# Layer 1's mixer in a decoder trunk: rows turned once, queries interleaved with compression, compressed heads summed in the turned result

## The reference

```python
s = modulate(rmsnorm(h, norm_kv), shift, scale)
kv = (s @ w_kv).reshape(B, S, 6, N_KV_GROUPS_B, HEAD_DIM)
k_cmp = rmsnorm(compress(kv[:, :, 0], pe_k, w_ck1, w_ck2), k_gains[0])
v_cmp = compress(kv[:, :, 1], pe_v, w_cv1, w_cv2)
k_sel = apply_rope(rmsnorm(kv[:, :, 2], k_gains[1]), cos, sin)   # v_sel, k_win, v_win likewise
proj = u @ w_in            # u: the same rows, other modulation
q = rmsnorm(proj[..., :hd].reshape(B, S, N_HEADS_B, HEAD_DIM), q_gain)
gates = jax.nn.sigmoid(proj[..., hd:] + b_gate).reshape(B, S, N_HEADS_B, 3)
q_rot = apply_rope(q, cos, sin)
p_cmp = jnp.where(vis, jax.nn.softmax(jnp.where(vis, logits, -1e30), axis=-1), 0.0)
o = gates[..., 0:1] * o_cmp + gates[..., 1:2] * o_sel + gates[..., 2:3] * o_win
return o.reshape(B, S, hd) @ w_o
```

## Time and profile before

| | |
|---|---|
| median of 3 runs | 1534.42 us (1533.08 to 1534.97) |
| profiled execution | 1527.08 us, its span 1525.4 us |
| PE busy | 1413.6 us (93%) |
| DVE, ACT busy | 328.9 us (22%), 266.6 us (17%) |
| DMA | 512.30 MB, mean 336 GB/s |
| mean granted clock of PE | 0.964 of full speed |

### The profile page before, as it was taken

How to read it: one execution, slowest core, us unless ns; L and a number is a source line. 1 busy time by engine, 2 the same in 40 slices (tenths; PEclk the granted TensorE clock), 3 DMA queues, 4 the chain that set the end, 5 groups by cost and what they waited for, 6 DMA issues and landing times.

```text
span 1525.4 us, 20445 instructions
## 1 busy us (share of the span) xinstructions
PE 1413.6 (93%) x8345; PEld 807.5 (53%) x8345; DVE 328.9 (22%) x774; ACT 266.6 (17%) x512; POOL 30.5 (2%) x77
## 2 busy tenths in 40 slices
PE   4999899999999999999797878889999999999997
PEld 1677766545444554444285757765454444544442
DVE  0330523211111111111132359232111111111111
ACT  2211513111111111111114236221111111111110
POOL 4000001000000000000000000010000000000000
PEclk7999999999999999999898959789999999999999
DMA  9999189599999999999976300124999999999996
GB/s 354 421 420 396 53 358 408 206 380 421 421 420 421 420 421 421 421 421 420 420 287 265 121 0 1 38 88 161 380 421 421 420 421 421 420 421 421 421 421 258
DMA packets 71311, 512.30 MB, mean 336 GB/s; under 512 B 8208, under 2 KB 8400, under 8 KB 9264
## 3 DMA queue, kind: packets, MB, share of 16 engines
q1 hardware_dynamic: 70272, 509.64, 81.3%
q0 software_dynamic: 800, 1.25, 0.4%
q10 hardware_dynamic: 144, 0.08, 0.0%
HBM read 509.89 MB, written 1.05 MB: 335 GB/s over the span
## 4 chain that ended last, share of the span: by engine, by line
PE 78%; DMA 13%; DVE 5%; ACT 2%; issue 1%; SPq 1%; DVEq 0%; ACTq 0%
PE PS L813 19%; PE PS L477 13%; DMA ring<-in_w_exp 11%; PE PS L803 10%; PE PS L821 10%; PE PS L836 9%; PE PS L498 3%; PE PS L865 2%; DMA ring<-in_w_ada_units 2%; PE PS L419 1%; PE PS L605 1%; PE PS L460 1%; DVE scratch L651 1%; DVE stats L654 1%; PE PS L904 1%
## 5 line engine op out<-in xcount | busy, mean ns | idle before, releaser
L813 PE MATMUL PS<-ring,scratch 128*32 128x512 f32 (+2 forms) x2176 | 359.3, 600 | 22.0 <-DMA ring<-in_w_exp 20.4
L813 PEld LDWEIGHTS PS<-ring,scratch 128*32 128x32 f32 (+2 forms) x2176 | 113.6, 123 | 261.3 <-issue 259.5
L477 PE MATMUL PS<-ring,uT 128*128 128x256 f32 x960 | 214.6, 383 | 1.9 <-ACT uT L443 1.1
L803 PEld LDWEIGHTS PS<-scratch,u 128*128 128x128 f32 x1600 | 183.2, 192 | 39.3 <-issue 37.4
L477 PEld LDWEIGHTS PS<-ring,uT 128*128 128x128 f32 x960 | 182.2, 192 | 34.0 <-issue 6.3
L803 PE MATMUL PS<-scratch,u 128*128 128x128 f32 x1600 | 192.4, 278 | 1.4 <-ACT scratch L1023 1.4
L821 PE MATMUL PS<-ring,scratch 128*32 128x512 f32 (+2 forms) x1088 | 182.2, 596 | 1.2 <-DVE item_first_i L1141 1.2
L836 PE MATMUL PS<-scratch 128*128 128x512 f32 x400 | 180.1, 593 | 0.0
L1156 DVE TENSOR_TENSOR scratch<-PS,gate_row 128x512 f32<-128x512 f32 x100 | 69.1, 691 | 446.7 <-PE PS L821 446.7
L1031 ACT ACTIVATE scratch<-PS 128x256 f32<-128x256 f32 x50 | 19.2, 383 | 676.0 <-PE PS L813 676.0
L821 PEld LDWEIGHTS PS<-ring,scratch 128*32 128x32 f32 (+2 forms) x1088 | 52.4, 122 | 123.1 <-issue 121.5
(11 more groups left out here) (301 smaller groups left out, 769.0 us busy)
## 6 DMA issues: line engine op xcount, KB each, us to landing
ring<-in_w_exp SPq DMA_DIRECT2D x384, 1024.0 KB, 21.1
ring<-in_w_ada_units SPq DMA_DIRECT2D x56, 1024.0 KB, 14.8
ring<-in_w_in_a_units SPq DMA_DIRECT2D x12, 1024.0 KB, 23.9
ring<-in_w_cmp_units SPq DMA_DIRECT2D x8, 1024.0 KB, 26.4
ring<-in_w_sh_units SPq DMA_DIRECT2D x6, 1024.0 KB, 9.9
ring<-in_w_kv_b_units SPq DMA_DIRECT2D x6, 1024.0 KB, 21.9
ring<-in_w_o_a_units SPq DMA_DIRECT2D x4, 1024.0 KB, 8.5
ring<-in_w_in_b_units SPq DMA_DIRECT2D x4, 1024.0 KB, 6.2
```

Source lines behind the costliest of these rows:

```text
L477: mm = pe_.matmul(PS[:, bank, t * UC:(t + 1) * UC], lhs[:, k, t * P:(t + 1) * P], w[:, k, :], start=(k == 0), stop=(k == KC - 1))
L803: mm = pe_.matmul(PS[:, bank, i * w:(i + 1) * w], u[:, t, k * P:(k + 1) * P], hot[:, t, :], start=(t == 0), stop=(t == NT - 1))
L813: mm = pe_.matmul(PS[places, GU, :], x[:, kk, places], gate_and_up, start=(kk == 0), stop=(kk == KC - 1))
```

## The change

- The normed rows are turned once. The keys' modulation writes `uT`; the queries' reads the same four banks and writes over `u` (`u_queries`), after all four banks are turned.
- Units are loaded and used in the order kv 0 to 3, compression 0 to 3, kv 4 and 5, compression 4 to 7, q 0 to 3. Plain and rotated queries are turned unit by unit (`turn_plain`, `turn_rotated`, four transpositions each), plain ones into `uT`, rotated ones into `qT`; DVE norms and rotates unit by unit. `dve_rope` handles both row tiles in one set of six operations.
- The gates' product comes after the last q unit.
- Scores and weights of the compressed branch are computed by DVE beside attention's batches 0 and 3, both row tiles at once, their exponentials by ACT after batch 1; each weight takes its gate with it. PE turns the probabilities with batches 6 and 7.
- The first branch's heads are written to `u` instead of being added. After attention `pe_turn_and_add` turns `u` by products with the identity, and adds the compressed heads in the same banks: eight products of 32 rows, 128x256 each.
- The masks `visible` and `hidden_mask` are made before the first kv unit's result is read.

```diff
-    order += [("kv", j) for j in range(6)] + [("cmp", j) for j in range(8)]
-    order += [("q", j) for j in range(4)] + [("out_b", j) for j in range(4)] + [("shared1", j) for j in range(3)]
+    order += [("kv", j) for j in range(4)] + [("cmp", j) for j in range(4)] + [("kv", 4), ("kv", 5)]
+    order += [("cmp", j) for j in range(4, 8)] + [("q", j) for j in range(4)] + [("out_b", j) for j in range(4)] + [("shared1", j) for j in range(3)]
...
+        def pe_turn_and_add(pe_, src, ready, what, added):
+            pe_.wait_ge(*ready)
+            for b in range(KC // 2):
+                for k in (2 * b, 2 * b + 1):
+                    place = PS[:, b, (k % 2) * SEQ:(k % 2 + 1) * SEQ]
+                    for t in range(NT):
+                        pe_.matmul(place[:, t * P:(t + 1) * P], src[:, t, k * P:(k + 1) * P], ident[:, :],
+                                   start=(k % 2 == 0 and t == 0), stop=False, skip_group_check=True)
+                    mm = added(k, place)
+                mm.then_inc(rows_turned, 1)
+            pe_.wait_ge(rows_copied, 4 * COPIED.index(what) + 4)
+
...
-        def act_modulate(done, what, v):
+
+        def act_modulate(done, what, v, dst=uT, in_place=False):
             done.eng.wait_ge(vectors_ready, 1 + [0, 1, 1, 2, 2][MODULATED.index(what)])
             for b in (0, 2):
-                done.eng.wait_ge(rows_turned, 4 * TURNED.index(what) + b + 1)
+                done.eng.wait_ge(rows_turned, 4 * TURNED.index(TURNED_FOR[what]) + (4 if in_place else b + 1))
...
+            kv(0)
+            pe_modulated(pe_, "mix1")
+            kv(1)
+            kv(2)
+            turn_doubled(0)
+            kv(3)
+            turn_doubled(1)
+            compress(0)
+            pe_.wait_ge(sem("kv_doubled"), 2)
+            kv(4)
             sum_tiles(0)
-            compress(1, 0)
-            compress(1, 1)
+            turn_doubled(2)
+            pe_.wait_ge(sem("kv_doubled"), 1)
+            kv(5)
+            compress(1)
+            turn_doubled(3)
+            pe_.wait_ge(sem("kv_doubled"), 3)
+            queries(0)
+            sum_tiles(1)
+            pe_.wait_ge(nsa_params, 16 * 2)
             pe_.wait_ge(sem("cmp_hidden"), 2)
             pe_.wait_ge(sem("kv_values"), 2)
...
-            compress(1, 2)
+            pe_.wait_ge(sem("kv_values"), 1)
+            queries(1)
             pe_.wait_ge(sem("cmp_k_normed"), 1)
...
                           ident[0:G * NB, 0:G * NB]).then_inc(sem("cmp_k_turned"), 1)
-            compress(1, 3)
-            sum_tiles(1)
+            pe_.wait_ge(sem("kv_copied"), 18)
+            turn_plain(0)
+            pe_.wait_ge(sem("kv_doubled"), 4)
+            queries(2)
+            turn_rotated(0)
+            turn_plain(1)
             pe_.wait_ge(sem("cmp_rep"), 2)
-            pe_.wait_ge(sem("kcz_ready"), 2)
...
-
-            pe_.wait_ge(sem("kv_doubled"), 4)
-            pe_.wait_ge(sem("kv_values"), 2)
+            pe_.wait_ge(sem("q_normed"), 1)
+            queries(3)
+            turn_rotated(1)
+            turn_plain(2)
             pe_.wait_ge(sem("kcz_ready"), 2)
-            pe_turn_rows(pe_, u, normed_rows("mix1"), "mix1")
-            pe_modulated(pe_, "mix1")
+            pe_narrow(pe_, w_gates, 6, u_queries, 3 * H, sem("gates_out"))
+            turn_plain(3)
+            turn_rotated(2)
+            turn_rotated(3)
+            pe_.wait_ge(sem("gates_active"), 1)
             pe_.wait_ge(sem("cmp_v_read"), 1)
-            pe_narrow(pe_, w_gates, 6, uT, 3 * H, sem("gates_out"))
-            for j in range(4):
-                pe_rows_unit(pe_, AT["q", j], j, uT)
-                if j == 0:
-                    pe_.wait_ge(sem("gates_active"), 1)
-                    pe_narrow_rows(pe_, narrow_T[0:3 * H, :], narrow_rows(6, SEQ, 3 * H)).then_inc(sem("gates_turned"), 1)
-            pe_turn_rows(pe_, q_rows, (sem("q_normed"), 4), "q")
...
+            def turn_cmp_probs(b):
+                t = b - CMP_TURNED_AT
+                if t in range(NT):
+                    pe_.wait_ge(sem("cmp_probs"), 1)
+                    return pe_.transpose(cmp_probs_turned(b), cmp_buf[:, t].rearrange("p h n -> p (h n)"), ident[:, :])
+
+            pe_.wait_ge(sem("rotated_copied"), 4)
             pe_attention(pe_, "nsa", nsa_batches, lambda br, pair: kT_b[:, br, pair // 2, :],
-                         lambda br, kt, hd: v_b[:, br, kt, hd // HPG, :])
-            pe_turn_rows(pe_, u, (sem("nsa_o"), 16), "nsa_o")
+                         lambda br, kt, hd: v_b[:, br, kt, hd // HPG, :],
+                         [(sem("cmp_shifted"), 1), (sem("gates_ready"), 1)], turn_cmp_probs)
+
+
+            def compressed_heads(k, bank):
+                rows = slice(32 * (k // 4), 32 * (k // 4) + 32)
+                return pe_.matmul(bank, v_diag[rows, 2 * (k % 4):2 * (k % 4) + 2, :].rearrange("p h d -> p (h d)"),
+                                  cmp_T[rows, :], start=False, stop=(k % 2 == 1), skip_group_check=True)
+
+            pe_turn_and_add(pe_, u, (sem("nsa_o"), 8), "nsa_o", compressed_heads)
...
+            act_head_squares(done, "kvn", 0, AT["kv", 2], KV_BANK[2], squares_kv)
+            to_compress(0)
+            values_of_branch(0)
+            to_compress(1)
             compressed(0)
+            act_head_squares(done, "kvn", 1, AT["kv", 4], KV_BANK[4], squares_kv)
             hidden_of(0)
+            keys_of_branch(0)
+            values_of_branch(1)
+            compressed(1)
+            keys_of_branch(1)
+            query_norm(0)
             act.wait_ge(sem("cmp_k"), 1)
             done(act.activation(kc_rows[0:G * NB, 0, :], PS[0:G * NB, 6, 0:DH], ACT.Square,
                                 accum_out=small[0:G * NB, 72:73]), sem("cmp_k_sq"))
             act.wait_ge(sem("cmp_k_mean"), 1)
             done(act.activation(small[0:G * NB, 74:75], small[0:G * NB, 73:74], ACT.Sqrt), sem("cmp_k_root"))
-            act_table(act, ACT.Silu)
-            compressed(1)
             hidden_of(1)
-            act_modulate(done, "mix1", OF_LAYER[1] + SH_M)
+            query_norm(1)
+            copy_plain(0)
+            query_norm(2)
+            copy_rotated(0)
+            copy_plain(1)
+            query_norm(3)
+            copy_rotated(1)
+            copy_plain(2)
             act.wait_ge(sem("gates_out"), 1)
             done(act.activation(narrow_T[0:3 * H, :], PS[0:3 * H, 6, 0:SEQ], ACT.Sigmoid, bias=bias_gate[:, :]),
                  sem("gates_active"))
-            for j in range(4):
-                act_head_squares(done, "qn", j, AT["q", j], j)
-            act_copy_turned(done, qT, "q")
+            copy_plain(3)
+            copy_rotated(2)
+            copy_rotated(3)
             act_table(act, ACT.Exp)
-            act.wait_ge(sem("cmp_shifted"), NT)
-            done(act.activation(cmp_buf, cmp_buf, ACT.Exp), sem("cmp_exp"))
-            act.wait_ge(sem("cmp_probs_turned"), 1)
-            done(act.activation(cmp_T[0:H * NB, :], PS[0:H * NB, 7, 0:SEQ], ACT.Copy), sem("cmp_probsT"))
-            act_copy_turned(done, qT, "q_rotated")
-            act_attention(done, "nsa", nsa_batches)
+
+            def cmp_exp(b):
+                if b == 1:
+                    act.wait_ge(sem("cmp_shifted"), 1)
+                    done(act.activation(cmp_buf, cmp_buf, ACT.Exp), sem("cmp_exp"))
+
+            act_attention(done, "nsa", nsa_batches, cmp_exp)
...
+            rotate(0)
+            query_norm(2)
+            rotate(1)
...
+            query_norm(3)
+            rotate(2)
+            rotate(3)
...
+            def cmp_scores():
+                dve.wait_ge(sem("cmp_logits"), 1)
+                done(dve.tensor_tensor(cmp_buf, cmp_logits, seen, ALU.mult))
+                done(dve.tensor_tensor(cmp_buf, cmp_buf, hidden_mask[:, :, :].unsqueeze(2).to_broadcast(of_heads), ALU.add))
+                done(dve.tensor_reduce(cmp_stat, cmp_buf, AX.X, ALU.max))
+                done(dve.tensor_tensor(cmp_buf, cmp_buf, cmp_stat.unsqueeze(3).to_broadcast(of_heads), ALU.subtract),
+                     sem("cmp_shifted"))
+
+
+            def cmp_weights():
+                dve.wait_ge(sem("cmp_exp"), 1)
+                done(dve.tensor_reduce(cmp_stat, cmp_buf, AX.X, ALU.add))
+                done(dve.reciprocal(cmp_stat, cmp_stat))
+                done(dve.tensor_tensor(cmp_stat, cmp_stat, gates[:, :, :].rearrange("p t (h b) -> p t b h", b=3)[:, :, 0, :],
+                                       ALU.mult))
+                done(dve.tensor_tensor(cmp_buf, cmp_buf, seen, ALU.mult))
+                done(dve.tensor_tensor(cmp_buf, cmp_buf, cmp_stat.unsqueeze(3).to_broadcast(of_heads), ALU.mult),
+                     sem("cmp_probs"))
+
+            def beside_attention(b):
+                if b == 0:
+                    cmp_scores()
+                elif b == 3:
+                    cmp_weights()
...
             def nsa_finish(b, heads, rinv):
                 br, t, g = nsa_batches[b]
```

(10 more changed lines are left out.)

336 lines of the change are left out of this document (173 added, 163 removed).

## The result

| | before | changed |
|---|---|---|
| median | 1534.7 us (1533.08 to 1535.22) | 1508.9 us (1505.23 to 1514.47) |
| ratio | | 0.984 (0.981 to 0.987) |
| profiled execution, its span | 1527.08, 1525.4 us | 1514.47, 1512.7 us |

The ratio times the 1534.4 us of the forecast gives 1509.7: faster, as forecast, but 9.4 us above the 1500.3 and just outside the range of 1491 to 1509. A second profile of the changed kernel, taken later (after_again), stands beside the first where that matters; its span is 1504.9 us, 20.5 less than before's.

What follows compares the result with a forecast made beforehand. Layer 1's mixer was taken as bound by PE's waits. Terms of -37.0, -3.0 and +5.9 sum to -34.1 us, giving 1493.0 profiled; adding 7.3 for the median gave 1500.3 us, range 1491 to 1509.

Steps and rivals of the forecast that it cites:

- What bounds it: Layer 1's mixer: bound neither by weights nor by PE's work, but by what PE waits for.
- the gain passes whole: After the mixer: its whole gain reaches the span's end, the rest staying 545.1 us, since PE's slot releases start the experts' weights.
- Part 1: First kv unit to attention's first logits: 97.2 us instead of 134.2, a gain of 37.0 us.
- the stall rival: Interleaved query units: ACT's in-order copies hold PE by 3 us in three units; 1509 us, chance 0.09.
- Part 2: Attention, first logits to the turning: DVE sets the pace; 64.1 us instead of 67.1, a gain of 3.0.
- I take full clock: Start of attention: PE enters from dense units at full clock, saving two waits (2.0 us) and half the first logits (0.5).
- DVE's terms: Attention: dropping the first branch's eight sums saves 3.7 us; eleven added DVE operations cost 3.2.
- Part 3: Turning the result, adding compressed heads, first out unit: 19.7 us instead of 13.8, a loss of 5.9; bounds 15.2 to 24.9.
- I take the slow stretch as long as today's: Turning: half clock ends 9.1 us after it begins, as before, so turning with heads takes 11.9 us.
- The second one: Rival: clock low entering attention (+2.0 us) and half clock through the turning and first out unit (+5.2); 1507.5 us, chance 0.17.
- The first rival: Attention's tail: the clock doesn't fall, turning stage 4.5 us less and last weighing 1.8 less; 1494 us, chance 0.13.
- The slower case: Interleaved stretch before attention: half its PE work at half clock undoes the gain; 1548 us, chance 0.03.

Runs made afterwards that it cites:

- e3: Changed kernel with the eight compressed-head products issued beside attention's last four batches, identity products then adding to them; 1493.9 us, ratio 0.976.
- e4: Changed kernel with compressed logits of three query units moved into the wait before the last rotated turnings, gates' product in bank 3; 1507.5 us, ratio 0.983.
- e13: Changed kernel plus eight dense 128x256 products, results written over, before the compressed logits; 1511.2 us, ratio 0.987.
- e6: Changed kernel plus the eight head products computed additionally in attention's tail, results written over, turning unchanged; 1503.7 us, ratio 0.983.
- e9: Changed kernel with the turning grouped after attention: first eight head products, then sixteen with the identity; 1496.2 us, ratio 0.976.
- e11: e3 with e4's edit and Sigmoid's table loaded before the gates' product is awaited; 1492.3 us, ratio 0.973.
- e5: Changed kernel with the compressed branch's weights made beside batch 7 instead of 3, turned with batches 9 and 10; 1514.4 us, ratio 0.986.
- e10: e6's extra head products in attention's tail, with the turning grouped as in e9; 1495.1 us, ratio 0.974.
- e12: e11 with the heads grouped after attention as in e9, instead of beside the last batches; 1495.8 us, ratio 0.976.
- e15: e9 with heads in the order 0, 4, 1, 5, 2, 6, 3, 7, so neighbours use different 32 rows; 1496.3 us, ratio 0.976.
- e14: Changed kernel with the two head products of each bank together, then its four with the identity; 1510.6 us, ratio 0.985.

## Why the prediction was right in sign and wrong in size

**What bounds it, and that the gain passes whole: right.** The rest of the span is 546.3 and 546.5 us against 545.1, and what e3 saves in turning and unit, 16.2 us, is in its span (1486.3 against 1504.9; 3.4 more come from the stage behind, 543.1 long, and 1.0 is lost by a later start). The experts' stretch from 1100 to 1500 is full as in the earlier trace rows: PE busy 388.6 us, DMA at 414 GB/s.

**Part 1: right, 1.2 us off in the second profile, 3.1 in the first.** In the second it is 98.4 against 97.2. The waits are as summed: 0.23, 0.77 and 1.17 for the last rotations and their copies, 2.2, against 1.7 + 0.6. What was missing is the clock at the end of the stage: the compressed logits took 5.62, not 4.05; in the first profile 6.92, and the stage 100.3. Before the last query unit no wait of PE was above 0.3 us, so the stall rival is out.

**Part 2: direction right, one term wrong.** "I take full clock" failed: the clock was 0.50 from 861 or 862 to 881 or 882 in both profiles of the changed kernel. It falls before attention's first logits (865 and 870), so attention isn't what makes this first fall, and dense units ahead don't keep it. Why it falls there is open: with 1.2 of the 1.9 us of waits filled it fell at 864.5 (e4), with dense products behind them at 868.8 (e13). DVE's terms held, in the groups of DVE's instructions from 870 to 939:

```profile
L2021 DVE TENSOR_TENSOR u<-u,scratch 128x256 f32<-128x256 f32 x8 | 3.4, 425 | 0.3
```

These are the second branch's eight sums; the first branch's eight, as long, are gone, 3.7 us with gaps. The eleven new operations are 3.15 us plus gaps. The result is 65.4, 1.3 above the forecast, or 68.1 where the clock fell once more at 892, behind PE's wait of 2.31 us.

**Part 3: the step that failed, 8.3 of the 10.8 us by which the three parts fell short in the second profile.** It was forecast at 19.7 us and took 28.0. Two of its terms were wrong, and its upper bound of 24.9 was too low because of the first. One: the prices were taken from products of the same size in rows of their own, 0.244 with the identity and 0.437 for a head. In alternation they are 0.32 and 0.63 at full clock (e6), and at half clock 1.15 for two and 1.15 for one in place of 0.98 and 0.87: 8 x 0.17 + 8 x 0.28 = 3.6 us. That 128x256 is the same size as a unit's product said nothing of 32 rows. Two: "I take the slow stretch as long as today's", 9.1 us. It lasted the whole 18.5 us and into the unit, 22 us from the first product. For a turning without alternation the same term would have held: with the heads grouped the clock was back after 7.7 to 9.3 us, and e9's stretch is 18.9 us long, near the 19.7 that was forecast. So what the forecast had wrong is that it took the order of the products as free. With the prices of the alternation, half clock throughout and the unit's measured 8.7, 18.5 + 0.75 + 8.7 is the 27.9 that was seen.

**The sum.** The sum of the parts gave 1493.0 for a profiled execution; the second profile was one of 1506.6, so it was 13.6 off: 10.8 in the three parts, 1.3 ahead of them, 1.4 behind. The forecast of the median was nearer, 5.4 and 8.6 us off, because 7.3 us were added for before's profiled execution being faster than its median. No run shows that such a difference belongs to the changed kernel: its second profiled execution was 0.9 us above its median, its first 5.6. That this term hid 7.3 us of the error is luck.

The product with the identity itself was priced rightly: sixteen of them, 32 records, took 3.84 us in e3, 0.24 a product at full clock, twice a transposition's 0.123. The Trainium skill (TensorE: Matmul & The Clock Gate, Terms) calls the transposing mode four times faster for FP32; by that the sixteen would take an estimated 7.9 us. The trace disagrees.

**Rivals.** The second one happened, both halves of it: low clock into attention and through part 3, forecast at 1507.5, measured 1505.7 and 1508.9. Its price for part 3, 5.2 us more, was too low by 3.1, and that its total agrees owes as much to the 7.3 us above. It had a chance of 0.17. In all eleven profiles whose tail holds no products of the heads, before's among them, the clock had fallen by the time the turning began, and the earlier trace rows had shown that; what was new is that it didn't come back. The likeliest case should have been that one. The first rival, no fall in the tail, occurred only in kernels that filled it. The slower case did not come near: the interleaved stretch is at 1.00 throughout.

**Open.** Whether alternation alone makes a full clock fall (e6, one profile) was not separated from the chance of that execution; e11 lost it at the same place without alternation. Why the alternation keeps the clock low though PE never waits isn't known either. What makes the clock come back 12 or 16 us after attention's first logits, and what brings the fall at 919 to 926 (e4, e5, e10, e12, e15), isn't known; attention's length, 65.4 to 77.7 us, moves more between the profiles than the start of the first kv unit, 765.1 to 770.3.

## What to carry to other kernels

Keep 32-row products from standing singly among 128-row ones: group them, put neighbours on different rows, or hide them in a stretch in which another engine sets the pace. Price a product from a row with its own number of rows and its own neighbours, not only its own output. Where the kernel before shows half clock behind a stage in which PE waits, take it as the likely case after the change too, and ask of the work that follows not only what it costs but whether the clock comes back in it.

## What was not expected of the hardware

- The clock did not come back during the alternation, though PE had no idle time: 18.5 us at 0.50. It came back in the first out unit behind it, or, with the heads grouped (e9), about 3 us after the last of them.
- A clock that came back 12 us after attention's first logits was lost again some 10 us later in all six such profiles, one that came back after 16 us was not (ten profiles).
- A 32-row product of 256 columns costs 0.47, 0.71, 1.0 or 1.15 us at half clock: rows in turn (e15), eight in a row with one change of rows (e9), in pairs on the same rows (e14, e10), alone between 128-row products.
- A filled tail of attention is hidden at full clock (65.4 us with and without) and is the bound at half: 76.7.
